# Two value chunks of an attention run as one product of 512 weight columns

## The chip, the core and the metric

The kernel is one program on one core of a Trainium2 chip. The metric is device time in microseconds (us) of that core, from the start to the end of one execution. Engines are named as in the profile: PE is TensorE's matmul side and PEld its weight loads, DVE is VectorE, ACT is ScalarE, POOL is GpSimd, and SP issues the big DMA loads.

## The reference, cut to what matters

The reference is a transformer layer with two attention branches and a gated feed-forward part (`first_block`), followed by two further layers (`second_block`). The change touches only the first projection of `first_block`, where the normed input `h` (256 tokens by 1024 features) is multiplied by `w_in` and cut into queries, keys and values of two branches:

```python
D_MODEL = 1024
SEQ = 256
def first_block(x, c, w_ada, ...):
    ...
        mod = c_act @ w_ada[l] + b_ada[l]
        sh_m, sc_m, gt_m, sh_f, sc_f, gt_f = jnp.split(mod, 6, axis=-1)
        h = modulate(rms_norm(x, g_mix[l]), sh_m, sc_m)
        proj = jnp.einsum('bsd,de->bse', h, w_in[l])
        qa, ka, va, qb, kb, vb, gate_logits = jnp.split(proj, splits, axis=-1)
        oa = moba_attention(to_heads(qa, N_HEADS_MOBA), to_heads(ka, N_HEADS_MOBA),
                            to_heads(va, N_HEADS_MOBA), rel_bias)
        ob = stick_breaking_attention(to_heads(qb, N_HEADS_SB), to_heads(kb, N_HEADS_SB),
                                      to_heads(vb, N_HEADS_SB))
        ya = jnp.einsum('bse,ed->bsd', merge_heads(oa), w_br_moba[l])
        yb = jnp.einsum('bse,ed->bsd', merge_heads(ob), w_br_sb[l])
        ...
        mixed = jnp.einsum('bsd,de->bse', g_a * ya + g_b * yb, w_out[l])
        x = x + gt_m[:, None, :] * mixed
        ...
def reference(...):
    x = first_block(...)
    return second_block(x, ...)
```

Each of qa, ka, va, qb, kb and vb has 512 columns. The products with `w_ada` (and, later, with the modulation weights of `second_block`) are products of one vector with a matrix.

## The kernel before

**Chunks.** All large weights lie in memory as blocks of 1 MB (128 partitions by 2048 numbers), 141 of them. 93 are "lin" chunks, each 256 columns of a weight matrix over all 1024 rows; 48 are "mod" chunks, for the vector products. `ORDER` fixes the order in which they come. Chunks 0 to 11 are the projection: 0 and 1 are qa, 2 and 3 ka, 4 and 5 va, and 6 to 11 the same for the second branch. From chunk 3 on, up to chunk 12, one mod chunk comes ahead of each lin chunk; none comes between 12 and 13.

**Three rings and who turns them.** SP loads chunk r into `raw[:, r % 4]` (L318) and first waits until DVE is done with chunk r - 4. For a lin chunk j, ACT then copies the raw numbers, rounded, to `w_hi[:, j % 3]` (L371), and DVE writes the remainder to `w_lo[:, j % 3]` (L865) and raises `lo_done`. A mod chunk is worked off by DVE alone, in two operations (L832), whose by-product goes into the slot of `w_lo` that the next lin chunk will fill. So both the copy of chunk j on ACT and the mod chunk ahead of it on DVE wait until PE has left slot `j % 3`, that is, until PE is done with chunk j - 3:

```python
if not isinstance(j, int) or j >= SPL:
    act.wait_ge(sem("lin_done"), LIN_OPEN + j - (SPL - 1))
nc.scalar.copy(w_hi[:, slot, :], raw[:, rslot, :]).then_inc(sem("hi_done"), 1)
```

(`LIN_OPEN` is 1 and `SPL` is 3; DVE's `mod` has the same wait.)

**PE** works chunk after chunk. Every product is done as three (`triple`: hi x hi, hi x lo, lo x hi), so a chunk is 2 halves x 8 row blocks x 3 = 48 matmuls of 256 columns. For queries and keys (`features`) the weights are stationary and the tokens stream; for values (`tokens`, chunks 4, 5, 10 and 11) the tokens are stationary and 256 weight columns stream. Chunk j writes PSUM bank `j % 2`, and waits for `lo_done` of chunk j and for ACT's copy of bank `j % 2` out of chunk j - 2 (`proj_evac`).

**ACT** runs a loop over j from 0 to 11 in which two things stand in a fixed order: first `split(j + 2)`, the copy to `w_hi` for chunk j + 2, then the copy of PSUM bank `j % 2` to `proj[:, j]` (L454), called the evacuation below. At j = 6 and 7 some small work is put in (L446 to L452). **DVE** runs only the splits in this stage, and after the one of chunk 13 it comes to the maxima of the first attention scores (L929).

**After chunk 11** PE waits for all twelve evacuations, does the scores of the first heads (L1435 to L1441), and then goes on with the chunks of the gates (12 to 19), between which the rest of the attention is spread.

Of the kernel before, what the change touches and what calls it, by code (L numbers as in the profile page):

```python
# [13 lines left out]
P = 128  # L14
T = 256
D = 1024
KT = D // P
# [105 lines left out]
def build(nc, xs_d, cond_d, vec_d, rel_d, w_d, fw_d, c0_d, c1_d, c2_d, c3_d, diff_d, out_d):  # L123
    ctx = ExitStack()
    with ctx:
# [5 lines left out]
        def sem(name):  # L131
            if name not in sems:
                sems[name] = ctx.enter_context(nc.semaphore(name))
            return sems[name]
# [115 lines left out]
        def halves(b):  # L250
            return b[:, 0:T], b[:, T:2 * T]
# [100 lines left out]
        def _(act):  # L352
# [89 lines left out]
            for j in range(LIN_GATE):  # L442
                split(j + 2)
                if j == 6:
                    act.wait_ge(sem("cond_loaded"), 16)
                    nc.scalar.activation(cond[:, :, :], cond[:, :, :], ACT.Silu).then_inc(sem("cond_ready"), 1)  # L446
                    load_ln_exp()
                if j == 7:
                    act.wait_ge(sem("c0_loaded"), 16)
                    act.wait_ge(sem("c1_loaded"), 16)  # L450
                    nc.scalar.copy(ident16, c0[:, C0["ident"]:C0["ident"] + P]).then_inc(sem("mask16_set"), 1)
                    nc.scalar.copy(past16, past).then_inc(sem("mask16_set"), 1)  # L452
                act.wait_ge(sem("lin_done"), LIN_OPEN + j + 1)
                nc.scalar.activation(proj[:, j, :], bank[j % 2][:, :], ACT.Copy,  # L454
                                     scale=QK if j % 6 < 2 else 1.0).then_inc(sem("proj_evac"), 1)

            act.dma_start(xs[:, :, T:2 * T], xs_d[:, :, T:2 * T]).then_inc(sem("ctx_loaded"), 16)

# [878 lines left out]
        def _(pe):  # L1337
# [3 lines left out]
            def triple(out, w, x, start, stop, skip=False):  # L1341

                for n, (a, b) in enumerate(((0, 0), (0, 1), (1, 0))):
                    last = mm(out, w[a], x[b], start=start and n == 0, stop=stop and n == 2, skip_group_check=skip)  # L1344
                return last

            def whl(slot, a, n):
                return w_hi[:, slot, a:a + n], w_lo[:, slot, a:a + n]

            def hhl(k, a, n):  # L1350
                return h_hi[:, k, a:a + n], h_lo[:, k, a:a + n]

            def features(j, slot, outs, a, n, order=None, ready=None):

                pe.wait_ge(sem("lo_done"), j + 1)
                order = order or [(k, k) for k in range(KT)]
                for m in range(2):
                    for i, (k, hk) in enumerate(order):  # L1360
                        if ready and m == 0:
                            ready(hk)
                        last = triple(outs[m], whl(slot, 256 * k + P * m, P), hhl(hk, a, n), i == 0, i == KT - 1)
                last.then_inc(sem("lin_done"), 1)

            def tokens(j, slot, outs, a):

                pe.wait_ge(sem("lo_done"), j + 1)
                for m in range(2):
                    for k in range(KT):  # L1370
                        last = triple(outs[m], hhl(k, a + P * m, P), whl(slot, 256 * k, 256), k == 0, k == KT - 1)
                last.then_inc(sem("lin_done"), 1)

            def sum_squares(name, ks=range(KT)):

# [32 lines left out]
            sum_squares("mix")  # L1408

            for j in range(LIN_GATE):  # L1410
                if j >= 2:
                    pe.wait_ge(sem("proj_evac"), j - 1)
                if j % 6 < 4:
                    features(j, j % SPL, halves(bank[j % 2]), 0, T, ready=tile_ready("mix") if j == 0 else None)
                else:
                    tokens(j, j % SPL, halves(bank[j % 2]), 0)

            def q_of(h, branch, a, b):
                t, p0 = h // 2, HD * (h % 2)
# [593 lines left out]
```

## Time and profile before

| | us |
|---|---|
| median of 3 runs (lowest, highest) | 795.64 (795.53, 795.8) |
| the profiled execution, its time | 795.57 |
| the profiled execution, its span in the trace | 793.8 |
| PE busy / DVE busy / ACT busy | 751.9 / 649.1 / 387.9 |

The span leaves out 1.8 us of the execution's own time. All times of rows are microseconds from the span's start. A matmul's row shows when it started and how long it took until its end came out; matmuls overlap, so the pace of PE is the distance from start to start. The stage that the change touches runs from 37.6 to about 110 us.

### The profile page before, as it was taken

What the parts mean: (1) busy time and instruction counts of PE and PEld (TensorE: products, weight loads), DVE (VectorE), ACT (ScalarE), POOL (GpSimd) and SP (SyncE); (2) the same over time, 40 slices, a digit from 0 to 9 for tenths busy, and PEclk for the clock granted to TensorE, in tenths of its full rate; (3) what the DMA queues carried; (4) which work ended last, traced back from release to release, by engine and by line L of the source; (5) the groups of instructions that cost most, each with busy time, mean ns of one, the idle gap of its engine ahead of it and who ended that gap; (6) DMA issues with size and microseconds to landing.
All of it is one profiled execution on the core that took longest, in us unless ns stands there. A gap on an engine that the chain in (4) does not pass through costs nothing.

```text
span 793.8 us, 13124 instructions
## 1 busy us (share of the span) xinstructions
PE 751.9 (95%) x5479; PEld 697.9 (88%) x5480; DVE 649.1 (82%) x1001; ACT 387.9 (49%) x521; POOL 46.2 (6%) x31
## 2 busy tenths in 40 slices
PE   0499999999999999999999999999999999999996
PEld 0399999999999999999999998888778899999995
DVE  3988767995897799999898779999989956987752
ACT  2355645557547654544547532322463335365742
POOL 0000000000000422223222000000000000000000
PEclk9799999999999999999999999999999999999998
DMA  9999998765563557766645241313106643563101
GB/s 347 417 352 365 368 348 311 264 223 198 206 240 136 208 212 251 273 246 247 258 175 197 91 176 53 107 55 104 54 0 235 224 148 118 225 231 118 54 1 54
DMA packets 26086, 156.58 MB, mean 197 GB/s; under 512 B 2691, under 2 KB 7084, under 8 KB 7852
## 3 DMA queue, kind: packets, MB, share of 16 engines
q1 hardware_dynamic: 21392, 148.91, 50.5%
q10 hardware_dynamic: 4636, 6.85, 2.6%
q8 instruction: 43, 0.70, 0.3%
q14 instruction: 15, 0.12, 0.0%
HBM read 154.68 MB, written 1.06 MB: 196 GB/s over the span
## 4 chain that ended last, share of the span: by engine, by line
PE 84%; DVE 9%; ACT 3%; issue 1%; ACTq 1%; POOL 1%; DVEq 0%
PE psum L1344 71%; DVE w_lo L832 4%; PE psum L1379 2%; DVE w_lo L865 2%; PE psum L1636 1%; PE psum L1810 1%; PE psum L1786 1%; ACT w_hi L371 1%; PE psum L1798 1%; PE psum L1622 1%; PE psum L1486 1%; DVE arena L1034 1%; DVE arena L1039 0%; PE psum L1601 0%; PE psum L1471 0%
## 5 line engine op out<-in xcount | busy, mean ns | idle before, releaser
L1344 PE MATMUL psum<-h_hi,w_hi 128*128 128x256 f32 (+1 forms) x1312 | 397.2, 303 | 10.2 <-DVE h_lo L905 9.2
L1344 PE MATMUL psum<-h_lo,w_hi 128*128 128x256 f32 (+1 forms) x1312 | 392.1, 299 | 0.0
L1344 PE MATMUL psum<-h_hi,w_lo 128*128 128x256 f32 (+1 forms) x1312 | 392.1, 299 | 0.0
L1344 PEld LDWEIGHTS psum<-h_hi,w_hi 128*128 128x128 f32 x1312 | 251.1, 191 | 21.8 <-issue 11.6
L1344 PEld LDWEIGHTS psum<-h_lo,w_hi 128*128 128x128 f32 x1312 | 251.5, 192 | 7.8 <-issue 0.2
L1344 PEld LDWEIGHTS psum<-h_hi,w_lo 128*128 128x128 f32 x1312 | 251.3, 192 | 7.4
L865 DVE TENSOR_TENSOR w_lo<-raw,w_hi 128x2048 fp32r<-128x2048 f32 x93 | 212.7, 2288 | 50.2 <-ACT w_hi L371 49.4
L371 ACT CAST w_hi<-raw 128x2048 fp32r<-128x2048 f32 x93 | 176.9, 1905 | 20.6 <-DMA raw<-in_w 16.3
L832 DVE SCALAR_TENSOR_TENSOR w_lo<-raw,cond 128x1024 fp32r<-128x1024 f32 x88 | 119.5, 1395 | 8.3 <-PE psum L1344 7.5
L832 DVE SCALAR_TENSOR_TENSOR w_lo<-raw,arena 128x1024 fp32r<-128x1024 f32 x48 | 56.8, 1221 | 0.8
L336 POOL TENSOR_TENSOR arena<-arena 128x512 f32<-128x512 f32 x11 | 26.1, 2370 | 372.9 <-ACT arena L588 372.9
L1344 PE MATMUL psum<-g_hi,w_hi 128*128 128x256 f32 x160 | 45.7, 286 | 1.7 <-POOL g_lo L339 0.9
L1090 DVE SCALAR_TENSOR_TENSOR arena<-att,vec,arena 128x256 f32<-128x256 f32 x116 | 47.0, 479 | 0.1
L1344 PE MATMUL psum<-g_lo,w_hi 128*128 128x256 f32 x160 | 45.3, 283 | 0.0
L1344 PE MATMUL psum<-g_hi,w_lo 128*128 128x256 f32 x160 | 45.3, 283 | 0.0
L560 ACT ACTIVATE arena<-psum,vec 128x256 f32<-128x256 f32 x44 | 22.4, 561 | 37.3 <-PE psum L1344 34.2
L388 ACT ACTIVATE att<-xs 128x256 f32<-128x256 f32 x32 | 12.4, 412 | 46.5 <-DVE xs L1197 24.1
L1344 PEld LDWEIGHTS psum<-g_hi,w_hi 128*128 128x128 f32 x160 | 30.6, 191 | 2.1 <-issue 1.1
L405 ACT ACTIVATE h_hi<-att,modv 128x256 fp32r<-128x256 f32 x48 | 23.0, 506 | 16.4 <-DVE att L899 16.4
L1344 PEld LDWEIGHTS psum<-g_lo,w_hi 128*128 128x128 f32 x160 | 30.6, 191 | 0.0
L1344 PEld LDWEIGHTS psum<-g_hi,w_lo 128*128 128x128 f32 x160 | 30.6, 191 | 0.0
L899 DVE SCALAR_TENSOR_TENSOR att<-xs,coef,rstd 128x256 f32<-128x256 f32 x40 | 20.4, 534 | 11.3 <-ACT rstd L398 11.1
(214 smaller groups left out, 783.7 us busy)
## 6 DMA issues: line engine op xcount, KB each, us to landing
raw<-in_w SPq DMA_DIRECT2D x141, 1024.0 KB, 4.9
xs<-in_xs ACTq DMA_DIRECT2D x2, 1024.0 KB, 12.0
consts<-diff ACTq DMA_DIRECT2D x8, 128.0 KB, 5.5
cond<-in_cond ACTq DMA_DIRECT2D x1, 1024.0 KB, 6.4
out<-xs SPq DMA_DIRECT2D x4, 256.0 KB, 2.4
arena<-in_cond ACTq DMA_DIRECT2D x1, 512.0 KB, 6.8
consts<-in_c ACTq DMA_DIRECT2D x1, 512.0 KB, 3.4
arena<-in_c ACTq DMA_DIRECT2D x1, 448.0 KB, 3.2
```

The lines of the kernel that those rows point to most:

```text
L336: nc.gpsimd.tensor_tensor(cv, cv, cg, ALU.mult).then_inc(sem("ffn_mult"), 1)
L371: nc.scalar.copy(w_hi[:, slot, :], raw[:, rslot, :]).then_inc(sem("hi_done"), 1)
L388: nc.scalar.activation(square_tmp(name)[:, k, :], xs[:, k, s * T:(s + 1) * T], ACT.Square).then_inc(sem(f"sq_{name}"), 1)
L405: nc.scalar.activation(h_hi[:, k, s * T:(s + 1) * T], norm_tmp[:, k, :], ACT.Identity, bias=shift_col(sh, k, v), scale=1.0).then_inc(sem(" ...
L560: nc.scalar.activation(dst[:, t, :], (src or bank[which])[:, t * T:(t + 1) * T], ACT.Identity, bias=col("b_conv", tile), scale=col("w_conv ...
L832: last = nc.vector.scalar_tensor_tensor(w_lo[:, slot, D * t:D * (t + 1)], raw[:, rslot, D * t:D * (t + 1)], 1.0, c, ALU.mult, ALU.mult, ac ...
L865: nc.vector.tensor_tensor(w_lo[:, slot, :], raw[:, rslot, :], w_hi[:, slot, :].bitcast(F32), ALU.subtract).then_inc(sem("lo_done"), 1)
L899: nc.vector.scalar_tensor_tensor(norm_tmp[:, k, :], xs[:, k, s * T:(s + 1) * T], coef[:, at + k:at + k + 1], rstd_of, ALU.mult, ALU.mult). ...
L1034: me.mark(nc.vector.scalar_tensor_tensor(dst[:, t, 1:T], src[:, t * T:(t + 1) * T - 1], col("w_conv", 44 + tile), dst[:, t, 1:T], ALU.mult ...
L1090: nc.vector.scalar_tensor_tensor(out, src, weight, acc, ALU.mult, ALU.add).then_inc(sem("conv_tap"), 1)
L1344: last = mm(out, w[a], x[b], start=start and n == 0, stop=stop and n == 2, skip_group_check=skip)
L1379: last = mm(bank[2 + s][:, s * T:(s + 1) * T], ones, square_tmp(name)[:, k, :], start=(k == 0), stop=(k == KT - 1))
```

## The change

In chunks 4 and 5, and again in 10 and 11, the two chunks are worked off together. PE waits for the weights of both, and for each half of the tokens does one product per row block whose streamed operand is a slice over two neighbouring slots of the ring (slots 1 and 2 each time), 2 x 256 columns. The half m of the tokens goes to bank m. `lin_done` is raised by two when both halves are done, and a new semaphore `values_half` is raised when the first is done. ACT's two evacuations of such a pair each take one half of the tokens for both chunks; the first waits for `values_half`, the second for the last `lin_done`.

```diff
@@ ScalarE, in the loop over j @@
-                act.wait_ge(sem("lin_done"), LIN_OPEN + j + 1)
-                nc.scalar.activation(proj[:, j, :], bank[j % 2][:, :], ACT.Copy,
-                                     scale=QK if j % 6 < 2 else 1.0).then_inc(sem("proj_evac"), 1)
+                if j % 6 < 4:
+                    act.wait_ge(sem("lin_done"), LIN_OPEN + j + 1)
+                    nc.scalar.activation(proj[:, j, :], bank[j % 2][:, :], ACT.Copy,
+                                         scale=QK if j % 6 < 2 else 1.0).then_inc(sem("proj_evac"), 1)
+                else:
+                    m, j0 = j % 2, j - j % 2
+                    if m:
+                        act.wait_ge(sem("lin_done"), LIN_OPEN + j + 1)
+                    else:
+                        act.wait_ge(sem("values_half"), j // 6 + 1)
+                    nc.scalar.copy(proj[:, j0:j0 + 2, T * m:T * (m + 1)], bank[m].rearrange("p (c n) -> p c n", c=2)
+                                   ).then_inc(sem("proj_evac"), 1)
@@ TensorE @@
-            def tokens(j, slot, outs, a):
-
-                pe.wait_ge(sem("lo_done"), j + 1)
+            def value_tokens(j):
+
+                pe.wait_ge(sem("lo_done"), j + 2)
+                slots = slice(j % SPL, j % SPL + 2)
                 for m in range(2):
+                    pe.wait_ge(sem("proj_evac"), j - 1 + m)
+                    out = bank[m].rearrange("p (c n) -> p c n", c=2)
                     for k in range(KT):
-                        last = triple(outs[m], hhl(k, a + P * m, P), whl(slot, 256 * k, 256), k == 0, k == KT - 1)
-                last.then_inc(sem("lin_done"), 1)
+                        w = w_hi[:, slots, 256 * k:256 * (k + 1)], w_lo[:, slots, 256 * k:256 * (k + 1)]
+                        last = triple(out, hhl(k, P * m, P), w, k == 0, k == KT - 1)
+                    if m:
+                        last.then_inc(sem("lin_done"), 2)
+                    else:
+                        last.then_inc(sem("values_half"), 1)
@@ TensorE, the loop over the chunks @@
             for j in range(LIN_GATE):
+                if j % 6 == 4:
+                    value_tokens(j)
+                if j % 6 >= 4:
+                    continue
                 if j >= 2:
                     pe.wait_ge(sem("proj_evac"), j - 1)
-                if j % 6 < 4:
-                    features(j, j % SPL, halves(bank[j % 2]), 0, T, ready=tile_ready("mix") if j == 0 else None)
-                else:
-                    tokens(j, j % SPL, halves(bank[j % 2]), 0)
+                features(j, j % SPL, halves(bank[j % 2]), 0, T, ready=tile_ready("mix") if j == 0 else None)
```

The instructions of ACT keep their places. These are its rows from the evacuation of chunk 8 to the first attention work, of the kernel before; the casts are the copies to `w_hi` for chunks 11, 12 and 13, and each `arena<-psum` row is one evacuation (chunks 8 to 11).

```order
L454 ACTIVATE arena<-psum 128x512 [waits lin_done]
L371 CAST w_hi<-raw 128x2048 [waits lin_done,arrived0]
L454 ACTIVATE arena<-psum 128x512 [waits lin_done]
L371 CAST w_hi<-raw 128x2048 [waits lin_done,arrived2]
L454 ACTIVATE arena<-psum 128x512 [waits lin_done]
L371 CAST w_hi<-raw 128x2048 [waits lin_done,arrived3]
L454 ACTIVATE arena<-psum 128x512 [waits lin_done]
L457 DMA xs<-in_xs 128x8x256
```

The same rows of ACT in the changed kernel:

```order
L455 ACTIVATE arena<-psum 128x512 [waits lin_done]
L371 CAST w_hi<-raw 128x2048 [waits lin_done,arrived0]
L455 ACTIVATE arena<-psum 128x512 [waits lin_done]
L371 CAST w_hi<-raw 128x2048 [waits lin_done,arrived2]
L463 COPY arena<-psum 128x2x256 [waits values_half]
L371 CAST w_hi<-raw 128x2048 [waits lin_done,arrived3]
L463 COPY arena<-psum 128x2x256 [waits lin_done]
L466 DMA xs<-in_xs 128x8x256
```

Nothing moved in the queue, but what the rows wait for did: the cast for chunk 13 (the one with arrived3) waits until chunk 10 has left slot 1, which is now the same event as the end of chunk 11, for which the row behind it waits too.

On PE the kernel before begins chunk 4, the first value chunk, like this; chunk 5 follows 48 rows later with the same wait.

```order
L1344 MATMUL psum<-w_hi,h_hi 128x256 [waits lo_done,proj_evac]
L1344 MATMUL psum<-w_lo,h_hi 128x256
L1344 MATMUL psum<-w_hi,h_lo 128x256
L1344 MATMUL psum<-w_hi,h_hi 128x256
L1344 MATMUL psum<-w_lo,h_hi 128x256
```

In the changed kernel the same place reads as follows; the only other wait of the pair stands 24 rows later and is for `proj_evac`, and chunk 6 begins after 48 rows.

```order
L1353 MATMUL psum<-w_hi,h_hi 128x512 [waits proj_evac,lo_done]
L1353 MATMUL psum<-w_lo,h_hi 128x512
L1353 MATMUL psum<-w_hi,h_lo 128x512
L1353 MATMUL psum<-w_hi,h_hi 128x512
L1353 MATMUL psum<-w_lo,h_hi 128x512
```

So 96 matmuls of 256 columns became 48 of 512, and the wait at the pair's start asks for one chunk more.

## Rows read from the trace of the kernel before

**Rows 1.** The chain that ended last, in order of time: start us, us, what.

```profile
37.61 71.76 PE psum L1344 x576
109.39 0.60 ACT arena L454
110.05 0.93 PE psum L1435 x8
```

**Rows 2.** Busy time by stretch: PE, PEld, DVE, ACT, POOL, then PEclk, DMA share, GB/s.

```profile
45.00:110.00 65.00, 64.36 (x535) 63.96 (x533) 51.10 (x53) 32.89 (x29) 0.00 (x0) 1.00 0.97 365
29.00:37.60 8.60, 0.00 (x0) 0.02 (x1) 8.14 (x19) 1.90 (x5) 0.00 (x0) 0.61 1.01 419
```

**Rows 3.** Timeline of PE (start us, us): first matmul of chunks 4, 6, 10; last.

```profile
63.12 0.28 PE L1344 MATMUL psum<-w_hi,h_hi 128*128 128x256 f32 x1
...
74.64 0.28 PE L1344 MATMUL psum<-h_hi,w_hi 128*128 128x256 f32 x1
...
97.68 0.28 PE L1344 MATMUL psum<-w_hi,h_hi 128*128 128x256 f32 x1
...
109.08 0.28 PE L1344 MATMUL psum<-w_hi,h_lo 128*128 128x256 f32 x1
```

**Rows 4.** Timeline of PE, first and last of 15 matmuls in a row, 512 columns.

```profile
485.73 0.39 PE L1344 MATMUL psum<-h_hi,w_hi 128*128 128x512 f32 x1
...
488.91 0.39 PE L1344 MATMUL psum<-h_hi,w_lo 128*128 128x512 f32 x1
```

**Rows 5.** Timeline of ACT: two casts together; for chunks 5, 11, 13; last evacuation.

```profile
41.48 3.71 ACT L371 CAST w_hi<-raw 128x2048 fp32r<-128x2048 f32 x2
...
59.83 1.91 ACT L371 CAST w_hi<-raw 128x2048 fp32r<-128x2048 f32 x1 [1.67 <-DMA raw<-in_w]
...
95.09 1.91 ACT L371 CAST w_hi<-raw 128x2048 fp32r<-128x2048 f32 x1 [2.37 <-DMA raw<-in_w]
...
104.13 1.89 ACT L371 CAST w_hi<-raw 128x2048 fp32r<-128x2048 f32 x1
109.39 0.60 ACT L454 ACTIVATE arena<-psum 128x512 f32<-128x512 f32 x1 [3.37 <-PE psum L1344]
```

**Rows 6.** Timeline of DVE: splits of 5, 9, 11, what follows each; first maxima.

```profile
61.85 2.29 DVE L865 TENSOR_TENSOR w_lo<-raw,w_hi 128x2048 fp32r<-128x2048 f32 x1 [0.41 <-ACT w_hi L371]
64.06 1.22 DVE L832 SCALAR_TENSOR_TENSOR w_lo<-raw,arena 128x1024 fp32r<-128x1024 f32 x1
...
85.63 2.29 DVE L865 TENSOR_TENSOR w_lo<-raw,w_hi 128x2048 fp32r<-128x2048 f32 x1 [2.35 <-ACT w_hi L371]
87.84 1.22 DVE L832 SCALAR_TENSOR_TENSOR w_lo<-raw,arena 128x1024 fp32r<-128x1024 f32 x1
...
92.46 1.22 DVE L832 SCALAR_TENSOR_TENSOR w_lo<-raw,arena 128x1024 fp32r<-128x1024 f32 x1
...
97.10 2.29 DVE L865 TENSOR_TENSOR w_lo<-raw,w_hi 128x2048 fp32r<-128x2048 f32 x1 [2.27 <-ACT w_hi L371]
...
112.52 1.02 DVE L929 TENSOR_REDUCE small<-psum 128x2 f32<-128x256 f32 x2 [4.17 <-PE psum L1441]
```

**Rows 7.** Loads into raw, 50 to 120 us, from issue to landing.

```profile
DMA to landing us min/median/max: 4.8/7.0/7.6
```

**Rows 8.** Busy time by stretch, as rows 2: PE goes idle, the clock follows.

```profile
28.60:29.60 1.00, 0.08 (x1) 0.00 (x0) 1.00 (x3) 0.85 (x2) 0.00 (x0) 1.00 0.97 390
...
30.80:31.40 0.60, 0.00 (x0) 0.00 (x0) 0.60 (x1) 0.00 (x0) 0.00 (x0) 0.57 0.99 410
...
40.60:41.20 0.60, 0.60 (x4) 0.53 (x4) 0.60 (x3) 0.32 (x2) 0.00 (x0) 0.56 0.95 396
```

**Rows 9.** Timeline of PE at the lower clock, the first of two triples.

```profile
37.61 0.55 PE L1344 MATMUL psum<-h_hi,w_hi 128*128 128x256 f32 x1 [8.93 <-DVE h_lo L905]
...
40.70 0.56 PE L1344 MATMUL psum<-h_hi,w_hi 128*128 128x256 f32 x1
```

**Rows 10.** Waits of PE: who for whom, us in total, times, longest.

```profile
PE psum L1344 <- DVE w_lo L865: 0.7, 1, 0.7
```

## The prediction

> **What bounds the kernel now.** I read the chain of waits first. It runs through PE without a break from 37.61 us over 576 matmuls, all twelve projection chunks, then through one evacuation, and back into PE [rows 1]. The table by stretches says the same: PE is busy for 64.36 of 65 us at the full clock, while DVE is busy 51.10 and ACT 32.89 [rows 2]. So in this stage a microsecond taken from PE's stream is a microsecond of the kernel, if the weights keep up. That is close: the loads fill 0.97 of the DMA engines at 365 GB/s in the same stretch, where 419 GB/s flowed ahead of it, with PE idle [rows 2]. After the stage PE stays the bound, with only small gaps, so I carry what the stage loses or wins to the end in full.
>
> **What the wide product saves.** PE's rows give its pace. From the start of chunk 4 (63.12) to that of chunk 6 (74.64) are 96 matmuls of 256 columns in 11.52 us, 0.120 each [rows 3]. The kernel has 512-column products of the same triples later: from 485.73 to 488.91 are 14 steps, 3.18 us, 0.227 each [rows 4]. A pair becomes 48 x 0.227 = 10.90 us. Saved: 0.62 us a pair, 1.24 in all. The halved count of weight loads brings nothing more, since loads lie beside matmuls in both cases. The 512 columns of those rows lie in one piece and those of the change in two slots, a form for which I have no row. Its bounds are the 0.227 of rows 4 and twice the 0.120 of rows 3, at which nothing would be saved and the sum below would be 1.2 us longer; I take the first, since there is one step in 512 columns. The Trainium skill, page "TensorE: Matmul & The Clock Gate", section "Back-to-back issue gap", gives two figures for 512 columns: 216 ns isolated and about 131 ns sustained. Row 4's stretch is a sustained one and agrees with the first; by the second a pair would take 6.3 us and the pairs would save 10.4 us, which is the last rival below. The reshaped evacuation writes the same 512 numbers per partition; I cost it as before, 0.60 [rows 5].
>
> **Wait 1, at the start of pair 4, 5.** It now needs `lo_done` of chunk 5. The split of chunk 5 starts at 61.85, and the next operation of DVE at 64.06 [rows 6], so it ends about 64.15; before it ACT's cast had waited for the load [rows 5]. Nothing of the change touches these, so PE, which would start at 63.12 [rows 3], starts at 64.2: **+1.08**. Pair 1 ends at 75.1, against 74.64 before.
>
> **Wait 2, at the start of pair 10, 11.** Slots 1 and 2 now come free together, at the end E of pair 1. Behind that wait stand, on DVE, mod 7 and the split of 7, and everything later; on ACT the cast of 7; on SP the loads that want their `raw` slots. Before, mod 7 could start when chunk 4 was done, 5.76 us earlier. So the head start of the weights is gone at E, and DVE has to do five mods and five splits (chunks 7 to 11) before pair 2, while PE does four chunks in 97.68 - 74.64 = 23.04 us [rows 3].
> - Lower bound: DVE never waits. One round is 92.46 - 87.84 = 4.62 us [rows 6]; 0.2 + 5 x 4.62 = 23.3, so PE waits 0.3.
> - Upper: the loads. Mod 7 is done at E + 2.6 and frees a slot for mod 9; the split of 7 is done at E + 4.8 and frees one for chunk 9. A load lands 4.8 us after its issue at least and 7.0 in the median of this stage [rows 7]. With cast and split behind it (1.9 + 2.2), chunk 9 is ready at E + 4.8 + 7.0 + 4.1 = E + 15.9; that frees the slot for chunk 11, which is ready at E + 15.9 + 11.1 = E + 27.0. PE waits 4.0.
> - Taken: landings of 5.9, midway. DMA has just stood idle, so the first is nearer 4.8, and the later ones queue again. Chunk 9 at E + 14.8, chunk 11 at E + 24.8: **+1.8**. The same chain is seen before, where chunk 11's cast waits for its load [rows 5] and its split starts at 97.10 [rows 6] and ends at 99.3, 1.6 us after the 97.68 at which a pair would have begun [rows 3].
>
> ACT's silu, which stands behind the cast of 8, lies under the wait for chunk 9's load and delays only the evacuation of 6, needed 11.5 us after E.
>
> **Wait 3, after pair 2.** ACT's queue holds the cast of chunk 13 ahead of the last evacuation. Before, that cast ran at 104.13, under chunk 11, and the evacuation began at 109.39, right at the end of the matmuls [rows 5]. Now the cast waits for `lin_done` of chunk 10, which comes with that of chunk 11. One cast, 3.71 - 1.91 = 1.80 us from start to start [rows 5], goes between PE's last product and the evacuation for which the attention scores wait: **+1.80** on PE's gap, which was 110.05 - 109.20 [rows 1, 3]. Nothing hides it: PE has no other work in its queue. DVE's split of 13 ends at about 4.3 us after the pair, the scores at 2.65 + 2.5 = 5.1 (112.52 - 110.05 for the second term [rows 6, 1]), so the maxima are not late a second time; that cover is 0.8 us. In the first pair the same order costs nothing, as chunk 6 needs only bank 0, and chunk 7 comes 5.8 us later.
>
> **Sum.** 1.08 - 0.62 + 1.8 - 0.62 + 1.8 = +3.4 us. Against the profiled execution's 795.57 (0.07 below the median): 799.0. With the bounds of wait 2: +1.9 to +5.6, 797.5 to 801.2. What a measurement of this kernel can tell from no change is about 0.2%, 1.6 us: 794.05 to 797.2.
>
> **The rivals.**
> - *The clock falls as well* (800.6). PE is idle some 1.8 us at wait 2 and 2.65 at wait 3. In the trace PE ran dry at 28.68 and the granted clock was at 0.50, 1.2 GHz, from about 30.88, 2.2 us later; it was back at 2.4 GHz at about 41.1, 3.5 us after work began [rows 8]. At the lower level 12 matmuls take 40.70 - 37.61 = 3.09 us [rows 9] instead of 1.44: +1.6. Against it: the gap must be as long as 2.2 us and fall badly, and only wait 3 is. The skill's section "What's actually happening" on the same page has the throttled state as the default that activity releases, which these rows bear out. Chance 0.20.
> - *The weights keep up* (797.5): wait 2 is only DVE's 0.3, landings near 4.8. For it: the loads have spare rate after E. Chance 0.12.
> - *No change that can be told* (796): part of the delay is taken back later, where PE now waits for weights that would then be ready, or wait 3 is hidden in a way that I don't see. Against it: of all PE's waits only one of 0.7 us ends with weights [rows 10], and all else that it waits for follows from its own products. Chance 0.08.
> - *Faster* (about 790): one mechanism, the streamed pace. If a 512-column product went at nearly the pace of one with 256 (0.12 us), a pair would take 5.8 us and save 5.8; with DVE's round of 4.62 against PE's 5.76 as the next bound over chunks 4 to 11, at most 8 x 1.14 = 9 us could be won, and waits 1 and 3 take 2.9 of that. It decides from a pace below about 0.17: then 96 x (0.240 - 0.17) outweighs 1.08 + 1.8 + 1.8 and the 1.6 of the bound. This is what the skill's 131 ns amounts to. Against it: 0.227 in 14 steps without a break [rows 4]. Chance 0.03.
>
> **How the numbers follow.** My forecast, the three waits at the full clock, has 0.57, its own range 797.9 to 800.0. The range 797.5 to 801.2 takes in that, the kept-up weights and the clock, and leaves out the last two rivals and some extreme of wait 2. Faster 0.03; same 0.09, the fourth case and a little of the third; slower 0.88.
>
> **What would show it.** Right: matmuls with 512 columns in two groups of 48, 0.227 apart; the first at about 64.2 behind DVE's w_lo, a second wait of 1.8 us before pair 2 near 98.1, released by w_lo and behind it a cast that waited for DMA; a PE gap of 2.65 us after pair 2 with a cast and then an evacuation in it; PE's stretches later as before but shifted by 3.4. A DMA share well below 0.97 in the few microseconds ahead of 78. Wrong: a pace other than 0.227 (wrong saving), pair 1 starting at 63.12, a second wait under 0.5 or over 3 us, a gap after pair 2 under 1.5, or a clock of 0.50 in the 3 us behind it.

## The result

The changed kernel is slower: 803.06 us median (800.52 to 805.65, 4 runs) against 795.67 (795.53 to 795.80, 4 runs) for the kernel before, ratio 1.0091, 95% interval 1.0075 to 1.0107. That is 7.4 us more at the median, where 3.4 were forecast, and outside the forecast range. The direction and the three waits were forecast; the size was not. The second fact is as telling as the first: in these four executions each, the kernel before repeats within 0.3 us, and the changed one varies by 5. Of the executions told below one, the fourth of e3, was disturbed (2616.87 us) and is left out.

The profiled execution is the shortest of the four, 800.52 us, with a span of 798.7 (before: 793.8). Its chain of waits, start us, us, what, from the first chunk on (L1353 are the projection's products, L1452 the attention scores, L463 the evacuation of a pair, L841 the mod chunks, L371 the casts, L874 the splits):

```profile
38.26 8.26 PE psum L1353 x48
...
62.12 2.30 DVE w_lo L874
64.46 11.21 PE psum L1353 x48
...
78.14 1.82 ACT w_hi L371
80.38 2.38 DVE w_lo L841 x4
...
85.00 2.38 DVE w_lo L841 x4
87.40 2.30 DVE w_lo L874
89.72 7.25 DMA raw<-in_w
96.99 1.92 ACT w_hi L371
99.00 2.30 DVE w_lo L874
101.35 11.19 PE psum L1353 x48
...
114.42 0.59 ACT arena L463
115.05 0.93 PE psum L1452 x8
```

Before, one row of PE, 71.76 us and 576 matmuls long, stood in this place [rows 1]. Now the chain leaves PE at both pairs: ahead of 64.46 it comes from the split of chunk 5, ahead of 101.35 from the load, cast and split of chunk 11, ahead of 115.05 from the last evacuation. PE's timeline has the three waits in brackets, and the pace of the wide product beside them:

```profile
64.46 0.50 PE L1353 MATMUL psum<-w_hi,h_hi 128*128 128x512 f32 x1 [0.54 <-DVE w_lo L874]
64.80 0.40 PE L1353 MATMUL psum<-w_lo,h_hi 128*128 128x512 f32 x1
...
74.82 0.39 PE L1353 MATMUL psum<-w_hi,h_hi 128*128 128x512 f32 x1
75.05 0.39 PE L1353 MATMUL psum<-w_lo,h_hi 128*128 128x512 f32 x1
75.27 0.39 PE L1353 MATMUL psum<-w_hi,h_lo 128*128 128x512 f32 x1
75.50 0.28 PE L1353 MATMUL psum<-h_hi,w_hi 128*128 128x256 f32 x1
...
101.35 0.50 PE L1353 MATMUL psum<-w_hi,h_hi 128*128 128x512 f32 x1 [2.66 <-DVE w_lo L874]
...
115.05 0.49 PE L1452 MATMUL psum<-arena 64*128 64x128 f32 x4 [2.53 <-ACT arena L463]
```

The pace is 0.227 us, as forecast. The start times, set against those of before [rows 1, 3], give the whole loss of this execution:

| PE starts | before | after | later by | forecast |
|---|---|---|---|---|
| chunk 0 | 37.61 | 38.26 | 0.65 | 0 |
| pair 1 (chunk 4) | 63.12 | 64.46 | 1.34 | 1.08 |
| chunk 6 | 74.64 | 75.50 | 0.86 | 0.46 |
| pair 2 (chunk 10) | 97.68 | 101.35 | 3.67 | 2.26 |
| the attention scores | 110.05 | 115.05 | 5.00 | 3.44 |

Behind that nothing is lost or won: the span grew by 4.9. The granted clock was at 1.00 from 43 us on. So this shortest execution is explained by the waits and the late start of chunk 0, with nothing slower behind them, and the rest up to 805.65 is something that this profile does not show.

In front of wait 2 the table by stretches shows what the loads did (PE, PEld, DVE, ACT, POOL, PEclk, DMA share, GB/s):

```profile
72.00:75.00 3.00, 3.00 (x15) 2.49 (x14) 0.00 (x0) 0.00 (x0) 0.00 (x0) 1.00 0.96 363
75.00:78.00 3.00, 3.00 (x24) 2.88 (x24) 2.25 (x3) 2.25 (x2) 0.00 (x0) 1.00 0.27 104
78.00:80.00 2.00, 2.00 (x19) 2.00 (x18) 1.97 (x3) 1.98 (x3) 0.00 (x0) 1.00 0.38 66
80.00:90.00 10.00, 10.00 (x85) 10.00 (x85) 9.93 (x12) 7.85 (x8) 0.00 (x0) 1.00 1.02 410
```

DVE and ACT stand idle while the pair holds slots 1 and 2 (0.00 in the first row), then the ring of `raw` is full and DMA falls to 0.27 and 0.38, and from 80 on it is busy all the time (1.02 at 410 GB/s) and stays behind.

### The profile page after: what moved, and what is told of

It reads as the page before. It is cut to its first block, busy times and chain, and to the rows that moved or that the text cites. A ratio compares the mean times of both kernels' runs of the same rounds, so it can differ in the third digit from the quotient of the medians.

```text
span 798.7 us, 12931 instructions
## 1 busy us (share of the span) xinstructions
PE 750.2 (94%) x5384; PEld 692.4 (87%) x5384; DVE 648.9 (81%) x1001; ACT 387.6 (49%) x521; POOL 46.2 (6%) x31
## 4 chain that ended last, share of the span: by engine, by line
PE 79%; DVE 11%; ACT 4%; issue 2%; DMA 2%; ACTq 1%; POOL 1%; DVEq 0%
PE psum L1353 66%; DVE w_lo L841 5%; DVE w_lo L874 3%; PE psum L1395 2%; DMA raw<-in_w 2%; ACT w_hi L371 2%; PE psum L1653 1%; PE psum L1827 1%; PE psum L1803 1%; PE psum L1815 1%; PE psum L1639 1%; PE psum L1503 1%; DVE arena L1043 1%; ACTq L358 1%; DVE arena L1048 0%
## 5 line engine op out<-in xcount | busy, mean ns | idle before, releaser
L1353 PE MATMUL psum<-h_hi,w_hi 128*128 128x256 f32 (+1 forms) x1312 | 397.3, 303 | 11.9 <-DVE h_lo L914 10.8
L1353 PE MATMUL psum<-h_lo,w_hi 128*128 128x256 f32 (+1 forms) x1312 | 392.2, 299 | 0.0
L1353 PE MATMUL psum<-h_hi,w_lo 128*128 128x256 f32 (+1 forms) x1312 | 392.1, 299 | 0.0
L1353 PEld LDWEIGHTS psum<-h_hi,w_hi 128*128 128x128 f32 x1312 | 251.3, 192 | 23.2 <-issue 13.3
L1353 PEld LDWEIGHTS psum<-h_lo,w_hi 128*128 128x128 f32 x1312 | 251.7, 192 | 7.8 <-issue 0.2
L1353 PEld LDWEIGHTS psum<-h_hi,w_lo 128*128 128x128 f32 x1312 | 251.5, 192 | 7.5
L874 DVE TENSOR_TENSOR w_lo<-raw,w_hi 128x2048 fp32r<-128x2048 f32 x93 | 212.6, 2287 | 53.8 <-ACT w_hi L371 53.0
L371 ACT CAST w_hi<-raw 128x2048 fp32r<-128x2048 f32 x93 | 177.0, 1906 | 33.0 <-DMA raw<-in_w 18.8
L841 DVE SCALAR_TENSOR_TENSOR w_lo<-raw,cond 128x1024 fp32r<-128x1024 f32 x88 | 119.5, 1394 | 8.3 <-PE psum L1353 7.5
L841 DVE SCALAR_TENSOR_TENSOR w_lo<-raw,arena 128x1024 fp32r<-128x1024 f32 x48 | 56.8, 1220 | 5.6 <-PE psum L1353 4.9
L1353 PE MATMUL psum<-g_hi,w_hi 128*128 128x256 f32 x160 | 45.7, 286 | 1.7 <-POOL g_lo L339 0.9
L1353 PE MATMUL psum<-g_lo,w_hi 128*128 128x256 f32 x160 | 45.3, 283 | 0.0
L1353 PE MATMUL psum<-g_hi,w_lo 128*128 128x256 f32 x160 | 45.3, 283 | 0.0
L1353 PEld LDWEIGHTS psum<-g_hi,w_hi 128*128 128x128 f32 x160 | 30.7, 192 | 2.1 <-issue 1.1
L1353 PEld LDWEIGHTS psum<-g_lo,w_hi 128*128 128x128 f32 x160 | 30.7, 192 | 0.0
L1353 PEld LDWEIGHTS psum<-g_hi,w_lo 128*128 128x128 f32 x160 | 30.7, 192 | 0.0
```

The source lines that it names most:

```text
L841: last = nc.vector.scalar_tensor_tensor(w_lo[:, slot, D * t:D * (t + 1)], raw[:, rslot, D * t:D * (t + 1)], 1.0, c, ALU.mult, ALU.mult, ac ...
L874: nc.vector.tensor_tensor(w_lo[:, slot, :], raw[:, rslot, :], w_hi[:, slot, :].bitcast(F32), ALU.subtract).then_inc(sem("lo_done"), 1)
```

## The experiments

Each run is one kernel beside the kernel before on the same chip; the line numbers shift a little from kernel to kernel.

**e1, the changed kernel again.**

> The changed kernel once more, unaltered, for its spread: it gave 800.5 to 805.7 us where the kernel before stays within 0.3 us. Theory A (waits and the clock): the three waits cost about 4.4 us at the full clock, and in some executions TensorE's clock falls to 1.2 GHz in or behind the gap after the second pair, so its times spread again from 800 to 806, and a run with a longer time has a lower mean granted clock; if the profiled one is a long one, its rows show a clock of 0.50 behind a wait, between 101 and 125 us. Theory B (loads): the spread comes from the landings that the second pair waits for; then the mean clock is the same in all and the wait ahead of pair 2 is as much longer as the run.

Measured: 804.32, 801.23, 802.61 and 804.95 us, ratio 1.0095 (1.0075 to 1.0114). This time the profile fell on a long one, 804.32. The same waits are there, 0.76, 2.69 and 2.53 us, and the clock is not at 1.00 (table by stretches, columns as above):

```profile
99.00:101.80 2.80, 0.43 (x4) 0.23 (x2) 2.42 (x3) 1.16 (x2) 0.00 (x0) 0.98 0.98 331
101.80:105.00 3.20, 2.88 (x7) 2.30 (x8) 2.55 (x5) 0.52 (x1) 0.00 (x0) 0.50 0.88 323
105.00:106.00 1.00, 1.00 (x6) 0.83 (x5) 0.00 (x0) 1.00 (x1) 0.00 (x0) 0.96 0.89 336
113.00:117.00 4.00, 1.67 (x8) 1.05 (x6) 0.31 (x1) 2.24 (x2) 0.00 (x0) 1.00 0.30 91
118.50:122.00 3.50, 3.50 (x16) 3.20 (x15) 2.08 (x4) 0.54 (x3) 0.00 (x0) 0.53 0.92 299
122.00:124.00 2.00, 2.00 (x18) 2.00 (x17) 1.96 (x6) 2.00 (x7) 0.00 (x0) 0.96 0.94 347
```

It fell to 0.50, 1.2 GHz, at the end of wait 2 and again behind wait 3. PE's first products of pair 2 run at that level: 0.43 us from start to start instead of 0.227.

```profile
102.12 0.80 PE L1353 MATMUL psum<-w_hi,h_hi 128*128 128x512 f32 x1 [2.69 <-DVE w_lo L874]
102.71 0.63 PE L1353 MATMUL psum<-w_lo,h_hi 128*128 128x512 f32 x1
103.14 0.63 PE L1353 MATMUL psum<-w_hi,h_lo 128*128 128x512 f32 x1
```

The price, from starts: pair 2 to the scores took 117.20 - 102.12 = 15.08 us, against 13.70 in the first profile, so 1.38 for the first fall. From the scores to the end of the span 802.5 - 117.20 = 685.30, against 683.65: 1.65 for the second. With the 0.77 by which pair 2 began later that is 3.80, which is 804.32 - 800.52. Theory B, the loads, has only the 0.77. The mean granted clocks of the eight executions of the changed kernel (four here, four in the result) go the same way: the four from 804.28 us up have 0.984 to 0.987, the three up to 801.83 have 0.990 to 0.992, and only 802.61, at 0.986, is out of order. It is a rough witness, since the mean also holds the stretch ahead of the first chunk, where a low clock costs nothing.

**e2, the pair's waits with products of 256 columns.**

```diff
                     pe.wait_ge(sem("proj_evac"), j - 1 + m)
-                    out = bank[m].rearrange("p (c n) -> p c n", c=2)
-                    for k in range(KT):
-                        w = w_hi[:, slots, 256 * k:256 * (k + 1)], w_lo[:, slots, 256 * k:256 * (k + 1)]
-                        last = triple(out, hhl(k, P * m, P), w, k == 0, k == KT - 1)
+                    for c, out in enumerate(halves(bank[m])):
+                        for k in range(KT):
+                            last = triple(out, hhl(k, P * m, P), whl((j + c) % SPL, 256 * k, 256), k == 0, k == KT - 1)
```

> All waits and slot releases of the change are kept, but each pair is done with 96 products of 256 columns instead of 48 of 512. Theory A: the product of 512 columns does save 0.62 us a pair, and only the waits cost; then this is 1.2 us slower than the changed kernel at its fastest, about 801.7, with the same spread upward. Rival C (the wide product over two slots is itself slow, because its operand lies in two places): this kernel is as fast as the changed one or faster.

Measured: 802.91 us median (802.80 to 808.40), ratio 1.0113 (1.0077 to 1.0149), beside 1.0095 for e1. The times of the two overlap, so they alone settle nothing; the profile does. Pair 1 takes from 63.83 to 75.44, 11.61 us, against 11.04 with the wide product at the same clock. The waits are those of the change (0.51, 2.91, 2.53), and the clock fell once, at wait 2: pair 2 to the scores took 15.81 us, 1.5 more than the 13.70 of the first profile with 0.62 for the narrow products. Without it this execution (802.90) would have been near the 801.7 expected. So the wide product isn't slow, and the coarser synchronisation makes a loss of this size without it. The one execution at 808.40, with a mean clock of 0.982 against 0.990, was not profiled.

**e3, the last evacuation first.**

```diff
             for j in range(LIN_GATE):
-                split(j + 2)
+                if j < 11:
+                    split(j + 2)
...
+                if j == 11:
+                    split(j + 2)
```

> The changed kernel with ScalarE's last evacuation (half 1 of chunks 10 and 11) put ahead of the cast of chunk 13. Theory A: wait 3 shrinks by 1.8 us, from about 2.5 to 0.7 us of idle TensorE, and with it the occasion for the clock to fall goes: 798.7 us, and a spread under 1 us. Theory B (spread from the loads ahead of pair 2): 1.8 us less in each run, 798.7 to 804, the spread as wide as before.

Measured: 800.52, 802.03 and 802.13 us, ratio 1.0073 (1.0056 to 1.009). Wait 3 went from 2.53 to 0.67, and from pair 2 to the scores it took 114.52 - 102.63 = 11.89 us instead of 13.70: 1.81, the one cast. The forecast total of 798.7 and the spread under 1 us were missed; by the totals alone theory B, 798.7 to 804, would do as well. The profiled execution (800.52, clock at 1.00) started its first chunk at 39.52, 1.3 us later than the changed kernel's, because two early loads for mod chunks came late; a cost from outside the change. And wait 2 was still 2.78.

**e4, a longer gap.**

```diff
                     if m:
                         act.wait_ge(sem("lin_done"), LIN_OPEN + j + 1)
+                        if j == 11:
+                            me.mark(nc.scalar.copy(att[:, 0:2048], att[:, 0:2048]))
+                            me.wait()
```

> The changed kernel with one more copy of 128x2048 on ScalarE (of a tile nobody uses then, onto itself) ahead of the last evacuation: wait 3 grows by about 1.9 us to 4.4. Theory A: the clock now falls in every execution; to the 1.9 us come 1.5 to 3.5 us of slow products, so all runs lie at 804 to 808 and the profiled one shows a clock of 0.50 from about 115 us on. Theory B: 1.9 us more in each run than the changed kernel, the clock stays at 1.00.

Measured: 807.29, 807.45, 806.30 and 805.31 us, ratio 1.0136 (1.0121 to 1.0151), within what theory A gave. Wait 3 is 4.46 us, wait 2 here 3.60, and the clock fell at both (0.50 from 104 to 106, 0.52 from 122 to 124). B's claim of a clock at 1.00 is out. That the clock fell in every execution, as theory A had it, is not shown: the one of 805.31 has a mean clock of 0.990, as high as the changed kernel's 800.52.

**e5 and e6, one pair each.** In e5 only chunks 4 and 5 are a pair, in e6 only 10 and 11; the other two use `tokens` and the old evacuation.

```diff
-                if j % 6 == 4:
+                if j == 4:
                     value_tokens(j)
-                if j % 6 >= 4:
+                if j in (4, 5):
                     continue
```

> Only chunks 4 and 5 run as a pair; 10 and 11 as before. Theory A: wait 1 (0.5 to 1.1 us) against 0.6 saved, and the missing head start is made up before chunk 11, since chunk 11 alone is needed 5.8 us later than a pair would need it. No wait is long enough for the clock. 795.6 to 796.8 us, spread under 1 us. Theory B (the emptied load queue by itself costs, pair or not): a wait ahead of chunk 10 or 11 and 798 or more.

Measured e5: 796.22 us median (795.82 to 798.67, 10 runs), ratio 1.0006 (0.9997 to 1.0015). The first pair alone costs nothing that can be told, though the interval reaches to 1.2 us and the profiled execution (796.65) comes to the scores 1.12 us late. PE waits 0.87 us ahead of the pair and then not again until the attention.

> Only chunks 10 and 11 run as a pair. Theory A: the weights of chunk 11 are ready at about 99.3, as before, so the wait ahead of the pair is 1.6 us instead of 2.7; wait 3 stays at 2.5 of idle TensorE. 1.6 - 0.6 + 1.9 = +2.9, 798.5 us at the full clock, and 800 to 801.5 where the clock falls in the gap behind the pair. Theory B: the wait ahead of the pair is 2.7 as in the changed kernel.

Measured e6: 800.01 us median (799.64 to 800.69), ratio 1.0051 (1.0037 to 1.0065). The wait ahead of the pair is 0.89 us, less than the 1.6 expected and not the 2.66 of the changed kernel:

```profile
98.86 0.50 PE L1353 MATMUL psum<-w_hi,h_hi 128*128 128x512 f32 x1 [0.89 <-DVE w_lo L874]
```

So the first pair adds 1.8 us to the wait ahead of the second, although alone it costs next to nothing. Behind wait 3 the clock fell in this profile:

```profile
112.50:117.00 4.50, 4.42 (x24) 3.85 (x25) 3.14 (x4) 0.24 (x2) 0.00 (x0) 0.69 0.91 297
```

**e7 and e8, three mod chunks moved.** e7 is e3 with the mod chunks ahead of chunks 5, 9 and 11 taken out and put ahead of 18, 19 and 20; e8 is the kernel before with the same order.

```diff
-        n = int(j >= 2) if j < LIN_GATE else 0 if j == LIN_GATE else 2 if j in (LIN_GATE + 2, LIN_GATE + 4) else int(j <= LIN_BR)
+        n = int(j >= 2 and j not in (4, 8, 10)) if j < LIN_GATE else 0 if j == LIN_GATE else 2 if j in (14, 16, 17, 18, 19) else int(j <= LIN_BR)
```

> The changed kernel with the last evacuation ahead of the cast of chunk 13, and with three mod chunks (those ahead of chunks 5, 9 and 11) moved to behind chunk 17, where DMA and VectorE have room. Theory A: 3 MB less to load and 7 us less of VectorE work lie in the stage, so waits 1 and 2 go, wait 3 is 0.7, and what is left is the product's saving: 1.2 us under its control e8 (the same order with 256-column products), spread under 1 us. Rival: the moved mods make VectorE late in the gate stage and give the time back there; then e8 is slower than the kernel before by as much.

> The kernel before with the same three mod chunks moved, as control for e7. Theory A: TensorE never waited for weights in the stage, so nothing is won there: 795.6 us, within 0.5. If VectorE gets late in the gate stage, 796 to 800.

Measured: e7 802.55 us median (802.18 to 803.88), e8 802.14 (802.10 to 803.43), ratios 1.0085 and 1.0081. In the stage itself e7 does what theory A says: PE has no wait ahead of either pair. Pair 1 takes 74.91 - 64.00 = 10.91 us, against 11.52 for its two chunks in e8 (63.13 to 74.65), and pair 2 up to the scores 109.69 - 97.94 = 11.75 against 110.05 - 97.69 = 12.36. The product saves 0.61 us a pair. In the total nothing of it is left (802.18 and 802.14 in the profiled executions), since the chain goes through VectorE later: e7 reaches the scores 0.36 us ahead of e8, and comes out of PE's long wait for VectorE 0.14 us behind it (189.07 against 188.93). The total is spoilt by the rival of that expectation: with the mods moved VectorE is late in the gate stage, in e8 as in e7. PE waits 3.7 us for it once (`att L971` in e8), the clock falls behind that wait, and it is at 0.97 on average between 180 and 240 us.

**e9, e10 and e11, another place for them.** The same three are put ahead of 18, 22 and 23. e9 has VectorE's split of 13 behind the first maxima as well as the early evacuation; e10 is the control without a pair; e11 is the changed kernel with the new order alone.

```diff
-        n = int(j >= 2) if j < LIN_GATE else 0 if j == LIN_GATE else 2 if j in (LIN_GATE + 2, LIN_GATE + 4) else int(j <= LIN_BR)
+        n = int(j >= 2 and j not in (4, 8, 10)) if j < LIN_GATE else 0 if j == LIN_GATE else 2 if j in (14, 16, 17) else 1
```

> The wide product with all three waits taken out: the mod chunks ahead of chunks 5, 9 and 11 are moved to behind chunks 17, 21 and 22 (in the gate stage VectorE then has no more to do than before up to chunk 20), the last evacuation stands ahead of the cast of chunk 13, and VectorE does the split of 13 behind the first maxima. Theory A: what is left is the product's saving of 1.2 us under the control e10, no clock falls, spread under 1 us: 794.5 to 795.5 us.

> Control for e9: the kernel before with the same three mod chunks moved and nothing else. Theory A: 795.6 to 796.2 us. If the later mods make VectorE late behind chunk 20: above 797, and e9 with it.

> The changed kernel with only the three mod chunks moved: waits 1 and 2 go, wait 3 stays at 2.5 us of idle TensorE. Theory A: e9 + 1.9 us at the full clock, 796.5 to 797.5, and 1.5 us more in those executions in which the clock falls in that one gap. It tells what waits 1 and 2 and the clock falls at them are worth: the changed kernel less this one.

Measured: e9 804.85 us median (802.89 to 806.47), e10 803.59 (802.18 to 804.97), e11 806.21 (805.01 to 807.30). All three expectations of the total were missed for the reason named in e10's: PE waits 5.3 us in three pieces for weights between 190 and 240 us in e10 (6.7 in e9), and the clock falls there. In e10 it fell behind both of the longer ones, 2.59 and 1.91 us. The stage repeats e7: pair 1 10.90 us, pair 2 to scores 110.20 - 98.46 = 11.74, no wait ahead of a pair. e11 keeps wait 3 at 2.53.

**e12, a longer program.** 96 matmuls of 8 columns stand behind PE's last one.

```diff
                 sum_squares("last", range(6) if m == 0 else (6, 7))
+            for _ in range(96):
+                mm(bank[3][:, 0:8], zeros[:, 0:P], zeros[:, 0:8], start=True, stop=True)
```

> The changed kernel with 96 matmuls of 8 columns put behind TensorE's last one, on a bank that nothing reads; they run while VectorE and the store end the kernel. It asks for the 0.65 us by which TensorE starts its first chunk later in the profiles of the kernels with both pairs wide (an early DMA issue of ScalarE, of the identity tile, takes 4.1 to 4.4 us there and 3.6 in the kernels with at least as many instructions as e5). If the length of TensorE's program decides it, this one issues in 3.6 us; if not, in 4.1 to 4.4 as the changed kernel.

Measured: one execution, 803.65 us, with clock falls at waits 2 (2.81) and 3 (2.53). ScalarE's early issue took 3.76 us, neither the 3.6 nor the 4.1 to 4.4 of the expectation but near the first, and chunk 0 started at 37.92.

```profile
2.98 3.76 ACTq L358 DMA_DIRECT2D c<-in_c  x1
```

In the changed kernel this row reads:

```profile
2.98 4.26 ACTq L358 DMA_DIRECT2D c<-in_c  x1
```

**e13, e14 and e15, mod chunks that don't wait for a slot.** The by-product of the mods ahead of chunks 3 to 12 goes to `att`, unused then. e13 has the early evacuation too, e14 not, and e15 is the kernel before with this edit.

```diff
+                early = isinstance(j, int) and SPL <= j <= LIN_GATE
                 dve.wait_ge(sem(f"arrived{rslot}"), arrived)
-                if not isinstance(j, int) or j >= SPL:
+                if early:
+                    dve.wait_ge(sem("norm_lo"), KT)
+                elif not isinstance(j, int) or j >= SPL:
                     dve.wait_ge(sem("lin_done"), LIN_OPEN + j - (SPL - 1))
...
-                            w_lo[:, slot, D * t:D * (t + 1)], raw[:, rslot, D * t:D * (t + 1)], 1.0, c, ALU.mult, ALU.mult,
+                            att[:, D * t:D * (t + 1)] if early else w_lo[:, slot, D * t:D * (t + 1)],
+                            raw[:, rslot, D * t:D * (t + 1)], 1.0, c, ALU.mult, ALU.mult,
```

> The changed kernel with the mod chunks ahead of chunks 3 to 12 writing their by-product into a tile that is unused then, in place of the slot of the next chunk (so they no longer wait for TensorE to leave it), and with the last evacuation ahead of the cast of chunk 13. Theory A (lost head start): mod 7 now runs, and frees its slot of raw, while the first pair is at work; wait 2 shrinks from 2.7 us to between 0.3 and 1.5, wait 3 to 0.7, the clock stays up: 796 to 797.5 us with a spread under 1.5 us. Rival (the loads' rate alone sets wait 2, whenever they start): wait 2 stays above 2 us, and some runs are 1.5 us longer by the clock, 798.5 to 802.

> As e13 but with the last evacuation where the change has it, so only wait 2 is treated. Theory A: e13 + 1.9 us where the clock stays up, 798 to 799.5, and 1.5 us more where it falls at wait 3. The changed kernel's highest times (above 803, two falls) are gone.

> Control: the kernel before with the mod chunks' by-product in the unused tile. TensorE doesn't wait in this stage, so 795.5 to 796.3 us, no change that can be measured.

Measured: e13 800.38 us median (799.10 to 801.27), ratio 1.0052 (1.0039 to 1.0064); e14 801.96 (800.17 to 805.78), 1.0088 (1.0062 to 1.0114); e15 795.78 (795.50 to 796.30), 0.9999 (0.999 to 1.0008). Mod 7 runs inside the pair now, and wait 2 is 2.02 in e13 and 2.10 in e14: shorter than 2.66 to 2.9, but by a quarter, not to the 0.3 to 1.5 expected. DVE's timeline of e13 tells why:

```profile
71.82 1.22 DVE L847 SCALAR_TENSOR_TENSOR att<-raw,arena 128x1024 f32<-128x1024 f32 x1
72.96 1.22 DVE L847 SCALAR_TENSOR_TENSOR att<-raw,arena 128x1024 f32<-128x1024 f32 x1
78.92 2.29 DVE L881 TENSOR_TENSOR w_lo<-raw,w_hi 128x2048 fp32r<-128x2048 f32 x1 [4.73 <-ACT w_hi L371]
```

The mod is done at 74, but the split of chunk 7 starts at 78.92 all the same, 2.3 us after the pair's end at 76.65, since its cast needs the slot. The release of `raw` for chunk 9 and then 11 hangs on that split. By its numbers the rival of that expectation, the loads' rate, did come in: a wait above 2 us, and times inside 798.5 to 802 for all five executions. But the rate alone isn't it, since the DMA engines were busy for only 0.05 of the time from 80 to 82 us, while the next load waited for the split of 7 to end at 81.1. From 84 on they are full, so both have a part, and no run here takes the rate by itself. Wait 2 did shrink, and even a wait of 2.02 let the clock fall in this profile (pair 2 to scores 13.45 us instead of e3's 11.89: 1.56). e14's longest time, 805.78, was expected not to occur; its profile is not of that run, so it stays unexplained.

## Why the prediction was wrong

**What held.** The forecast was three waits made by the coarser synchronisation against a small saving, slower by more than can be overlooked. *Pace of the wide product*: 0.227 us, and 0.61 us saved a pair without a wait ahead (e7); with one, the first products go 0.1 us slower in all and 0.5 are saved. That the slice over two slots costs nothing is shown, but no two kernels here show the saving in the total clear of the spread. The 131 ns of the Trainium skill, page "TensorE: Matmul & The Clock Gate", section "Back-to-back issue gap", are not seen: the products of 512 columns go at 0.227 us in rows 4, in e7 and in the changed kernel. *Wait 1*: forecast 1.08; it is +0.69 beyond the late start of chunk 0, of which PE stood idle for 0.54. *Wait 3*: forecast 1.80; e3 takes it away and gives 1.81. *The order of the queues* (one cast ahead of the evacuation, two slots released together) is behind waits 3 and 2, as e3 and e6 show; wait 1 is the pair's need of chunk 5's weights.

**The step that failed first: the clock.** I gave its fall a chance of 0.20, allowed it for wait 3 only, once, and set the forecast at the full clock, because the one fall in the trace came 2.2 us after PE ran dry and only one wait was longer. In the profiles of the change and its relatives, 14 waits at the pair or behind it are 2.0 to 2.9 us long, and the clock fell at 7 of them; both longer ones (e4) had it; none of 1.0 us or less did.

| profile | wait 2 | clock | wait 3 | clock |
|---|---|---|---|---|
| change | 2.66 | stays | 2.53 | stays |
| e1 | 2.69 | falls | 2.53 | falls |
| e2 | 2.91 | falls | 2.53 | stays |
| e3 | 2.78 | stays | 0.67 | stays |
| e4 | 3.60 | falls | 4.46 | falls |
| e6 | 0.89 | stays | 2.53 | falls |
| e11 | none | stays | 2.53 | stays |
| e12 | 2.81 | falls | 2.53 | falls |
| e13 | 2.02 | falls | 0.68 | stays |
| e14 | 2.10 | stays | 2.53 | stays |

The moved mods of e7 to e11 made waits in the gate stage, and they fit in: it fell at four of the five from 1.91 to 2.59 us (e9, e10, e11) and at all three from 3.41 to 3.74 (e7, e8, e9). The cost is 1.4 to 1.7 us each, as rows 9 gave it. With two such waits in every execution, one fall is the likely case and two are common, which gives 802 to 804 where no fall gives 800.5. Of the 4.0 us between the forecast (799.0) and the median, 1.5 stand in the profile without a fall, and the other 2.5 are of the size of one to two falls. The prediction's own sign of being wrong, a clock of 0.50 in the 3 us behind wait 3, stands in e1's profile. What I should have read from rows 8 is that one fall, 2.2 us after PE ran dry, tells how late a fall can come in one case, and not that a shorter wait is safe.

**The second: the size of wait 2.** Taken 1.8, measured 2.81 from the starts. The term that was off is "landings of 5.9, midway" for both loads. The first, chunk 9, landed 5.0 us after its slot was free (80.4 to 85.39); the second, chunk 11, took 7.4 (89.6 to 96.99), above the stage's median of 7.0. I had written that the later ones queue again and still took the mean for both. That makes 0.6 us more than two landings of 5.9. The rest, some 0.5 us, is in the hand-offs: 0.1 us more than taken up to the free slot, 0.1 behind the first landing and 0.3 behind the second. e6 shows the dependence on the first pair: 0.89 us of wait without it, 2.66 with it. e13 confirms the part of the mod chunk, about a quarter, and its rows show the split of 7 still behind the pair; how the larger part divides between that slot and the loads' rate is not shown.

**The third, not in the sum: 0.65 us at the start.** The changed kernel's chunk 0 starts later because ScalarE's early DMA issue of the tile of constants (L358) takes 4.26 us, 3.58 in the kernel before, and all behind it is later. In the profiles it takes 4.1 to 4.4 in every kernel with 96 matmuls fewer on PE (the change, e1, e3, e4, e7, e9, e11, e13, e14) and 3.6 to 3.7 in those with 48 fewer or none (before, e2, e5, e6, e8, e10, e15); 96 put back at the end (e12) give 3.76. So it goes with the number of matmuls in PE's program, and not with the waits. Why, no run here tells.

**What stays open.** Waits, start and two falls make 804.3; single executions at 805.65 (the change), 805.78 (e14) and 808.40 (e2) lie above, and none of them was profiled. Late early loads, as in e3's profile (1.3 us), could fill the gap. So could the stretch at 1.2 GHz with which chunk 0 begins, which the forecast took as fixed: the clock was back at 41.1 us before and only at about 44.4 in e9, where chunks 0 to 3 took 26.14 us without a wait ahead of chunk 4, against 25.51 before. Or there were more falls, as the mean clocks of 0.985 (805.65) and 0.982 (808.40) suggest, against 0.987 in e1's profile with two. Waits of the same length (2.53 us) now lose the clock and now don't; what decides it isn't shown.

## What to carry to other kernels

Before merging two steps of a ring, list what each old release let begin, on every queue: with two of three slots released together, the cast, the vector work and the loads lose their head start at once, and a ring deep enough for single steps is too shallow for double ones. Look at what stands ahead of an evacuation in its queue, since a wait that used to be long over can become the same event as the one behind it. And where TensorE has run without a break, a new idle time of two microseconds is to be priced with the slower clock behind it, which here cost 1.4 to 1.7 us in about half of the cases. A product that is faster by itself can still save nothing in the total: e7 had its two pairs without a wait, and lost the gain at a wait further on.

## What the runs showed that was not expected

The time varies from execution to execution, in good part with the clock's falls: 5 us of spread for the changed kernel, 0.3 for the kernel before beside it, and at most 1.4 for the kernel before beside the later experiments. Idle time of 1.91 us was followed by a fall in one profile (e10), 2.78 was not in another (e3). Taking the places of three mod chunks out of the stage and putting them behind chunk 17 or later cost 6 to 8 us without any pair (e8, e10), though VectorE was busy for only 11.25 of the 20 us from 180 to 200 in the kernel before. And the early DMA issue of ScalarE changes by 0.5 to 0.8 us with the number of matmuls in TensorE's program.
